# A decoder layer with expert retrieval on one core: mixer and routing steps moved in front of the dot product in VectorE's order

## What is computed

```python
h = modulate(rms_norm(x, g_norm1), shift1, scale1)
proj = h @ w_in                                  # a | u | v
mixed = concat([pool_mixer(a), spatial_gating(u, v)])
x = x + gate1 * (mixed @ w_out)
h = modulate(rms_norm(x, g_norm2), shift2, scale2)
q = h @ w_query                                  # 8 heads, 2 sides of 128
scores = einsum('thpd,hpkd->thpk', q, sub_keys)
s_top, i_top = top_k(scores, 16)                 # of 128 keys a side
best, sel = top_k(s_top[0][:, None] + s_top[1][None, :], 16)
idx = ...                                        # 16 of 16384 experts a head
act = gelu(einsum('thkd,td->thk', expert_down[idx], h))
x = x + gate2 * einsum('thk,thkd->td', softmax(best) * act, expert_up[idx])
out = rms_norm(x, g_final)
```

## Time and profile before

| | |
|---|---|
| median of 3 runs | 2860.85 us (2857.14 to 2862.76) |
| the profiled execution | 2857.36 us, its span 2855.6 us |
| mean granted clock of TensorE | 0.699 of full speed |
| TensorE, matmuls | 1962.8 us busy (69%) |
| VectorE | 1917.2 us (67%) |
| ScalarE | 1210.1 us (42%) |
| GpSimd | 1121.9 us (39%) |
| moved by DMA | 1166.39 MB, mean 408 GB/s |
| chain that ended last | DMA 53%, TensorE 22%, VectorE 13%, ScalarE 6%, issue 3% |

### The profile page before, as it was taken

The page is one execution under the profiler, slowest core; times in us unless marked ns, Lnnn a source line. Parts: engine busy times, 40 slices in busy tenths (PEclk is TensorE's granted clock), DMA queues, the critical chain, the costliest instruction groups (busy, mean ns, idle before and its releaser), DMA issues.

```text
span 2855.6 us, 37916 instructions
## 1 busy us (share of the span) xinstructions
PE 1962.8 (69%) x12940; PEld 898.9 (31%) x12940; DVE 1917.2 (67%) x4729; ACT 1210.1 (42%) x3860; POOL 1121.9 (39%) x1032
## 2 busy tenths in 40 slices
PE   5798898877976676665666767665666666666554
PEld 4454453443542332231322323231322322232110
DVE  5876676775767466677676756677676866676554
ACT  1245454464453344444344444444344544444333
POOL 0033333444434244444444444444444444444332
PEclk9897898888977567665766656565666657565555
DMA  9799999999999999999999999999999999999997
GB/s 404 284 370 397 399 419 403 402 420 412 419 408 398 419 420 421 421 421 421 420 421 420 417 416 413 422 421 421 421 406 421 418 421 405 422 421 421 421 421 311
DMA packets 170230, 1166.39 MB, mean 408 GB/s; under 512 B 19123, under 2 KB 25779, under 8 KB 36790
## 3 DMA queue, kind: packets, MB, share of 16 engines
q0 software_dynamic: 147456, 1073.81, 91.2%
q1 hardware_dynamic: 22582, 90.17, 8.0%
HBM read 1156.03 MB, written 7.86 MB: 408 GB/s over the span
## 4 chain that ended last, share of the span: by engine, by line
DMA 53%; PE 22%; DVE 13%; ACT 6%; issue 3%; SPq 2%; POOL 0%; DVEq 0%; POOLq 0%; ACTq 0%
DMA work<-experts,expert_rows 41%; DMA weights<-experts,expert_rows 8%; PE ps_sum L803 7%; DVE work L1418 6%; PE ps_small L769 4%; PE ps_m L711 3%; DMA work<-w_ada 2%; PE ps_wide L743 2%; PE ps_m L655 2%; PE ps_m L666 1%; ACT weight L1008 1%; ACT diag L1013 1%; DMA vn_u<-x_scratch 1%; SPq L569 1%; PE ps_m L675 1%
## 5 line engine op out<-in xcount | busy, mean ns | idle before, releaser
L607 POOL DMA_INDIRECT work<-experts,expert_rows x930 | 1022.0, 1099 | 1559.6 <-PE ps_sum L803 1393.6
L1418 DVE CUSTOM_DVE_ANT_0 work<-work 128x1024 f32<-128x1024 f32 x930 | 1135.6, 1222 | 727.9 <-DMA work<-experts,expert_rows 726.4
L803 PE MATMUL ps_sum<-work,diag 128*32 128x256 f32 x7440 | 826.1, 529 | 724.7 <-ACT diag L1013 722.5
L1006 ACT ACTIVATE act_out<-act_in 128x1 f32<-128x1 f32 x1024 | 207.5, 203 | 1177.6 <-DVE act_in L1418 1174.3
L803 PEld LDWEIGHTS ps_sum<-work,diag 128*32 128x32 f32 x7440 | 171.6, 127 | 1266.5 <-ACT diag L1013 1189.8
L1013 ACT ACTIVATE diag<-const,weight 128x32 f32<-128x32 f32 x1024 | 329.1, 321 | 33.5
L1008 ACT ACTIVATE weight<-gate,act_out 128x1 f32<-128x1 f32 x1024 | 301.6, 295 | 33.2
L769 PE MATMUL ps_small<-h_t,weights 128*128 128x128 f32 x1344 | 300.6, 393 | 0.0
L769 PEld LDWEIGHTS ps_small<-h_t,weights 128*128 128x128 f32 x1344 | 257.8, 286 | 132.4 <-issue 126.3
L743 PE MATMUL ps_wide<-h_cur,const 32*128 32x512 f32 x260 | 205.9, 882 | 0.8 <-ACT work L979 0.8
L803 PE MATMUL ps_sum<-weights,diag 128*32 128x256 f32 x752 | 89.4, 563 | 107.0 <-ACT diag L1013 99.3
(11 more groups left out here) (175 smaller groups left out, 1674.6 us busy)
## 6 DMA issues: line engine op xcount, KB each, us to landing
work<-sides SPq DMA_DIRECT2D x44, 576.0 KB, 8.4
work<-w_ada SPq DMA_DIRECT2D x12, 2048.0 KB, 23.5
work<-experts,expert_rows POOLq DMA_INDIRECT x930, 15.7
weights<-sides SPq DMA_DIRECT2D x16, 576.0 KB, 37.6
weights<-w_in SPq DMA_DIRECT2D x3, 2048.0 KB, 17.1
x_buf<-x SPq DMA_DIRECT2D x8, 512.0 KB, 11.4
weights<-w_out SPq DMA_DIRECT2D x2, 2048.0 KB, 35.7
x_scratch<-h_buf SPq DMA_DIRECT2D x7, 512.0 KB, 8.2
```

Source lines behind the costliest of these rows:

```text
L607: nc.gpsimd.indirect_dma_start(ring[x.ring], None, experts, bass.IndirectOffsetOnAxis(ap=rows_flat[:, x.column:x.column + 1], axis=0),).th ...
L803: last = nc.tensor.matmul(ps_sum[quarter(c), x.group, :], diag[:, x.ring, :], ring[x.ring][:, D + c * QCOLS:D + (c + 1) * QCOLS], start=x. ...
L1006: nc.scalar.activation(act_out[:, s:s + 1], act_in[:, s:s + 1], ACT.Gelu).then_inc(s_gelu, 1)
L1418: nc.vector.tensor_tensor_reduce(down, down, h2_spread[x.segment % 2], 1.0, 0.0, ALU.mult, ALU.add, act_in[:, x.g % TURN:x.g % TURN + 1]). ...
```

## The change

In VectorE's loop over the slots the mixer's and the routing's steps of a slot are issued in front of the slot's dot product, not behind it. `place_choices` stays behind it, as do all other steps. Which slot a step belongs to is unchanged, and so are the other engines' programs.

```diff
             for x in TABLE:
+                for tile, n in mixer_steps(x.g):
+                    mixer(n, tile)
+                for e in range(1, TURNS):
+                    n = x.g - ROUTE_AT[e]
+                    if 0 <= n < ROUTE_STEPS:
+                        route_step(n, e + 1)
                 dot(x)
...
                 if x.g in SCALE_W_SLOTS:
                     scale_w_out(SCALE_W_SLOTS.index(x.g))
-                for tile, n in mixer_steps(x.g):
-                    mixer(n, tile)
                 if x.tile + 1 < TILES and x.s == PREP_AT[x.tile] + STATS2:
                     stats2(x.tile + 1)
                 if x.tile + 1 < TILES and x.s == PREP_AT[x.tile] + NORM2:
                     norm2(x.tile + 1)
                 for e in range(1, TURNS):
-                    n = x.g - ROUTE_AT[e]
-                    if 0 <= n < ROUTE_STEPS:
-                        route_step(n, e + 1)
                     if x.g - 1 == WIDE_AT["moved", e + 1]:
                         place_choices(e + 1)
```

## The result

The changed kernel took 2888.05 us (median of 4 runs, 2887.04 to 2895.33); the kernel before, run beside it, 2858.99 (4 runs, 2853.9 to 2862.76). The ratio is 1.011, with a 95% interval of 1.0096 to 1.0124: **29 us slower**. Forecast were 8, with a range up to 2876. The profiled execution took 2888.2 us, its span is 2886.4 and the mean granted clock 0.707.

The account below looks back on a forecast made before the run. The prediction took the DMA transfers, chiefly the 1024 gathers, to set the time. Its terms 3.4 + 2.9 + 1.2 + 0.8 = 8.3 us on 2859.5 gave 2867.8, forecast as 2867.5 us, range 2857 to 2876.

Parts of the forecast that it names:

- the gathers' waits for the expert product: Sign in the changed profile: these waits grow by about 3 us before 220 us.
- Place 1: Slots 0 to 16: VectorE late behind the wait for v's root, TensorE's output product starts late, costing 3.4 us.
- place 2: Slots 32 to 48: waits for reciprocal and statistics hold dot products back; 4.0 us less 1.1 backlog, 2.9 us.
- place 3: Slots 50 to 66: the wait for the scores comes first, output product starts 2.1 us late; less 0.9 backlog, 1.2 us.
- The remaining tiles: Fourth dip (660 to 680 us) and all later places: later dot products mostly go unnoticed, 0.4 us each, 0.8 us.
- In a run of steps without waits: VectorE's order: steps and dot products still alternate, covered by the wait for rows, so this costs nothing.
- A delay of TensorE: At the next dip in DMA share, a delay costs only what exceeds the backlog of queued gathers.
- upper bound of 11.9: Most the change could cost, in us: all delays with no backlog deducted, 3.4 + 4.0 + 2.1 + 2.4.
- The waits: VectorE's waits for the statistics of v on TensorE would grow from 10.1 to about 17 us.
- (a): Rival: backlog and other transfers cover the delays; 0 to +5 us, 2860 to 2865, no change; chance 0.40.
- (b): Rival: steps fit into waits for rows, VectorE gets ahead and fills the dips; 2856 or 2854; chance 0.06.
- (c): Rival: longer idle time carries TensorE's lower clock into the output product; 8 to 12 us on top, about 2877; chance 0.10.

Follow-up runs that it names:

- e13: The whole change against the kernel before, but with window sums, means and gating left behind the dot product: 2877.58 us against 2859.79, ratio 1.0065.
- e9: Kernel before with only first norm's reciprocal, statistics of v, scaling of v and residual moved in front of the dot product: 2861.72 us against 2858.5.
- e16: Kernel before plus four scratch additions in front of seven dot products that TensorE takes up late: 2860.61 us against 2859.58, ratio 1.0002.
- e10: Kernel before with only window sums, means and gating moved in front of the dot product: 2871.12 us against 2858.5, ratio 1.0051.
- e12: Kernel before with the window sums alone moved in front of the dot product: 2864.73 us against 2859.79, ratio 1.0017.
- e15: Kernel before plus four scratch additions in front of seven dot products that TensorE follows at once, output product next: 2874.23 us against 2859.58, ratio 1.0051.
- e17: Kernel before plus four scratch additions in front of seven dot products that TensorE follows at once, no output product next: 2862.49 us against 2859.58.
- e7: Kernel before with five ring buffers instead of six up to slot 267: 2889.7 us against 2856.79, ratio 1.0111.
- e8: Changed kernel with five ring buffers up to slot 267, against the kernel before: 2908.02 us, ratio 1.0175.
- e2: Kernel before with only the routing's steps moved in front of the dot product: 2868.77 us against 2859.35, ratio 1.0034.
- e14: Kernel before with routing step 0 alone moved in front of the dot product: 2862.37 us against 2859.79, ratio 1.0014.
- e1: Kernel before with only the mixer's steps moved in front of the dot product: 2871.58 us against 2859.35, ratio 1.0037.
- e4: Kernel before with only reciprocal, statistics and scaling of v, window sums, residual and routing step 0 moved in front: 2872.57 us, ratio 1.005.
- e3: The change, but reciprocal, statistics and scaling of v, window sums, residual and routing step 0 stay behind, against the kernel before: 2871.35 us, ratio 1.0045.
- e11: The kernel of e3 once more on another chip, against the kernel before: 2873.52 us against 2858.5, ratio 1.0051.

## Why the prediction was right or wrong

**Right.** What bounds the kernel, that nothing changes from 935 us on, that only the dot product behind a step is at stake, and the sign. Most of the named signs came: the reciprocal of v's root waits 2.57 us instead of 0.37, the DMA share of the first 100 us from 137 us on falls from 0.97 to 0.93, the first routing step's waits came to 23.3 us, over 12. One did not: the gathers' waits for the expert product before 220 us were forecast to grow by about 3 us and went from 49.9 to 50.6.

**Near in size, and in part by luck.** Place 1, forecast 3.4, had a lag of 5.6 at slot 18 and 4.1 at slot 30; place 2, forecast 2.9, added 3.7 up to slot 42. The waits in them are those forecast, place 1's of 2.57 us and place 3's of 3.58 (forecast 3.6):

```profile
149.33 0.17 DVE L1226 RECIPROCAL stat<-stat 128x1 f32<-128x1 f32 x1 [2.57 <-ACT stat L943]
...
299.93 0.87 DVE L1315 MAX8 top_s<-wide 128x8 f32<-128x128 f32 x4 [3.58 <-ACT wide L992]
```

But e13, the change without the run of window sums, means and gating, stands at 2.6 us at slot 18 and 3.2 at slot 42, where the whole change has 5.6 and 7.8. So about half of what looks like places 1 and 2 belongs to the window sums of slot 12, which were priced at nothing. And e9, which has the single mixer steps of all seven tiles in front, cost 3 us in all.

**Wrong: "The remaining tiles. The same waits recur, but the landing times around them are mostly 9 us and more, and where TensorE lags by 2 to 5 us the later dot product is not noticed", 0.8 us.** The lag grew from 11.4 at slot 72 to 31.7 at slot 270, by 20.3 us. This term holds most of the error. The second half of the sentence is true (e16), and the landing times were read rightly (10.7 us in the median from 137 to 935 us, in the trace of before), but they did not protect; the window sums, means and gating stand where TensorE does not lag: in the trace of before the products of slots 91 to 93, 130 to 133 and 172 to 174 end within 1.2 us of the end of their diagonal.

**Wrong: "In a run of steps without waits this is the same alternation with another beginning, and costs nothing; what covers it is the wait for rows."** The run alone costs 13 us (e10). Two things were missed. The list of waits was taken from what waited before; the window sums waited for 1.5 us there because a dot product ran ahead of them, and without it they wait for 14.8. And a step in front of a dot product that TensorE is already waiting for delays it by its own length, wait or no wait, and this stays where the output product follows (e12 against e10, e15 against e17).

**Wrong: "A delay of TensorE costs what it exceeds the backlog by, at the next dip."** The backlog, landing time less 5.7 us, is no store that can be spent for nothing: e7 lost 33 us with landing times of 9.2 us in the median and a share of 0.98. The rate is lower whenever fewer gathers are in flight, which the share hides. With this the upper bound of 11.9 was none.

**Place 3**, forecast 1.2 us, went from 7.8 at slot 42 to 14.2 at slot 66 and 11.4 at slot 72, so 3.6 to 6.4. Its wait was right; the window sums of slot 52 were not in it (e13 goes from 3.2 to 8.0 and 5.4 at the same slots).

**The waits** of the statistics were forecast at about 17 us and came to 30.9, since VectorE now reaches them one dot product earlier at every tile. Long as they are, they cost little.

**The rivals.** (a) and (b) are out by the interval. (c) is out too: the granted clock from 137 to 935 us is 0.86, not below the 0.85 of the earlier trace rows, and the four matmuls of the output product still take 1.88 us. The rule of the Trainium skill that stood beside (c) (TensorE: Matmul & The Clock Gate, HAM oscillation — how this bites in real kernels) makes the group behind such a wait slow each time. The trace agrees in part: behind 1 us or more of idle time the slot's expert product was slow, mostly 1.08 us, in 40 of 54 cases before and in 32 of 52 after the change (137 to 935 us), and fast, mostly 0.64, in the others, as behind the 3.88 us above. Slow products were 66 before and 65 after in all, so nothing of the loss lies there.

**Open.** Why e8 lost only 18 us over e7. And what the routing's steps 1 to 18 cost by themselves: e2 less e14 gives them 6 to 7 us, and they wait for nothing, so I take it to be their length ahead of dot products that TensorE is waiting for, as with means and gating; this was argued and not tried. Nor do the parts add up exactly: e1 and e2 make 22 us, e10 and e13 make 30, the change 29, each with an interval of some 4 to 5 us to either side.

## What to carry to other kernels

Before moving a step in front of work that another engine waits for, look not at how long the step waits today, but at what that engine does at that place and after it. If it lags, the delay is nearly free (1 of 19.3 us in e16). If it takes up the result at once and a stretch without gaps follows there, most of the delay passes through, the step's wait and its length alike (15 of 19.3 in e15). If it takes it up at once and has gaps afterwards, most is caught up again (3 of 19.3 in e17). A short wait in a profile says nothing about the wait that comes once the work ahead of it is taken away. For a kernel bound by its DMA engines, compare the bytes moved by a given time: a busy share near 1 doesn't show that nothing is lost.

## What was not expected of the hardware

A DMA share of 0.98 to 1.01 goes with rates from 386 to 421 GB/s. The mean packet of 8 KB took 322 ns before and 330 after the change in the stretch from 137 to 935 us, though fewer gathers were in flight, and some 315 in the faster stretch behind it (own count over the packets of 8192 bytes).

In the profiles of e1 to e4 and of e15 to e17 VectorE has 9 to 18 us of idle time that the profile puts down to issue, mostly some 1 us ahead of a dot product; those of before, after and all other experiments have none. The number of VectorE's instructions is the same in e1 to e4. e3's repetition (e11) took as long without them, and e16 took as long as before with 18.0 us of them: they cost nothing that could be seen, and their cause stays open.
